# A two-layer encoder trunk on one core: the first layer's attention as one pipeline of paired heads

## The reference

```python
h = x @ w_in
q_lat, ckv, krope, g_mla, dq, dk, dv, g_diff = split(h)       # 256, 128, 32, 512, 512, 512, 512, 512 columns
q = (rmsnorm(q_lat) @ w_uq)                                    # 8 latent heads of 64 + 32 (rope)
ckv = rmsnorm(ckv); krope = rope(krope); dq, dk = rope(dq), rope(dk)
# latent attention, 8 heads: softmax(q_abs . ckv + q_rope . krope) @ ckv, then @ w_uv
# differential attention, 4 heads with two maps each:
a = softmax(q1 . k1) - lam * softmax(q2 . k2);  o_diff = rmsnorm(a @ v) * (1 - lam_init)
o = concat([o_mla * silu(g_mla), o_diff * silu(g_diff)]) @ w_out
y = layernorm(ALPHA * x + o)
```

## Time and profile before

| | |
|---|---|
| time, median of 3 runs (lowest, highest) | 985.28 us (981.5, 987.18) |
| the profiled execution: time, span | 975.73 us, 973.9 us |
| mean granted TensorE clock | 0.957 |
| PE, DVE, ACT, POOL busy (share of the span) | 90%, 58%, 41%, 6% |
| the chain that ended last: PE, issue, DVE, ACT | 64%, 20%, 6%, 4% |
| DMA, mean | 88 GB/s |

### The profile page before, as it was taken

The page is one execution under the profiler, slowest core; times in us unless marked ns, Lnnn a source line. Parts: engine busy times, 40 slices in busy tenths (PEclk is TensorE's granted clock), DMA queues, the critical chain, the costliest instruction groups (busy, mean ns, idle before and its releaser), DMA issues.

```text
span 973.9 us, 17284 instructions
## 1 busy us (share of the span) xinstructions
PE 881.3 (90%) x6744; PEld 745.6 (77%) x6744; DVE 561.7 (58%) x1189; ACT 398.3 (41%) x836; POOL 54.3 (6%) x75
## 2 busy tenths in 40 slices
PE   4897989999998998998989999999999999898975
PEld 3896568788877765786779999888888888766653
DVE  3166533644462676557595246657656666778867
ACT  3232331222232443424113265566557555755520
POOL 0001000000000000000022001000100010000001
PEclk9899979899999998999999999999999999999978
DMA  7232010211224234014203333323332343234301
GB/s 252 67 87 62 1 55 29 67 37 40 71 66 153 71 114 127 24 46 152 83 25 103 107 112 101 121 85 113 116 110 89 110 121 115 63 101 135 97 38 70
DMA packets 70606, 86.14 MB, mean 88 GB/s; under 512 B 8208, under 2 KB 57120, under 8 KB 70528
## 3 DMA queue, kind: packets, MB, share of 16 engines
q1 hardware_dynamic: 67632, 76.76, 25.7%
q0 software_dynamic: 2896, 8.28, 2.4%
HBM read 74.12 MB, written 10.90 MB: 87 GB/s over the span
## 4 chain that ended last, share of the span: by engine, by line
PE 64%; issue 20%; DVE 6%; ACT 4%; SPq 2%; POOL 2%; DMA 2%; DVEq 0%; POOLq 0%; ACTq 0%
PE turn L858 21%; PE pair L858 19%; PE proj L858 9%; PE value L858 9%; PE turn L896 1%; POOL rstd L831 1%; DVE w_lo L1439 1%; PE turn L1064 1%; PE value L896 1%; DMA stage<-in_w_out_even_dram 1%; PE pair L896 1%; SPq L678 1%; ACT w_hi L1247 1%; PE proj L896 1%; DMA stage<-in_w_in_even_dram 1%
## 5 line engine op out<-in xcount | busy, mean ns | idle before, releaser
L1439 DVE TENSOR_TENSOR w_lo<-stage,w_hi 128x512 fp32r<-128x512 f32 (+1 forms) x144 | 96.7, 683 | 149.8 <-ACT w_hi L1247 149.1
L858 PE MATMUL turn<-w_hi,xT_hi 128*128 128x256 f32 (+2 forms) x430 | 137.6, 320 | 4.8 <-DVE xT_lo L1444 1.8
L858 PE MATMUL turn<-w_lo,xT_hi 128*128 128x256 f32 (+2 forms) x430 | 133.1, 309 | 0.0
L858 PE MATMUL turn<-w_hi,xT_lo 128*128 128x256 f32 (+2 forms) x430 | 132.8, 309 | 0.0
L1247 ACT CAST w_hi<-stage 128x512 fp32r<-128x512 f32 (+1 forms) x144 | 86.7, 616 | 47.9 <-DMA stage<-in_w_in_even_dram 14.9
L858 PEld LDWEIGHTS turn<-w_hi,xT_hi 128*128 128x128 f32 x430 | 85.1, 198 | 10.0 <-DVE xT_lo L1444 2.1
L858 PEld LDWEIGHTS turn<-w_hi,xT_lo 128*128 128x128 f32 x430 | 84.8, 197 | 3.6
L858 PEld LDWEIGHTS turn<-w_lo,xT_hi 128*128 128x128 f32 x430 | 85.1, 198 | 2.9
L858 PE MATMUL pair<-w_hi,xT_hi 128*128 128x256 f32 (+2 forms) x196 | 59.8, 305 | 9.9 <-DVE w_lo L1439 9.9
L1317 ACT ACTIVATE probs<-pair,stats 128x272 f32<-128x272 f32 (+4 forms) x64 | 33.1, 518 | 86.9 <-DVE stats L1547 86.6
L1558 DVE TENSOR_TENSOR_SCAN probs<-probs 128x512 f32<-128x512 f32 (+4 forms) x80 | 60.9, 794 | 1.6
(11 more groups left out here) (509 smaller groups left out, 2099.7 us busy)
## 6 DMA issues: line engine op xcount, KB each, us to landing
stage<-in_w_in_odd_dram SPq DMA_DIRECT2D x64, 256.0 KB, 2.7
stage<-in_w_in_even_dram SPq DMA_DIRECT2D x44, 256.0 KB, 2.8
k_c<-in_cache_sb_k_dram SPq DMA_DIRECT2D x32, 256.0 KB, 3.4
v_c<-in_cache_sb_v_dram SPq DMA_DIRECT2D x32, 256.0 KB, 2.9
x_sb<-in_x_prompt_dram SPq DMA_DIRECT2D x8, 512.0 KB, 4.4
mlaK<-in_cache_diff_k_dram SPq DMA_DIRECT2D x8, 512.0 KB, 3.7
mlaK<-in_cache_diff_v_dram SPq DMA_DIRECT2D x8, 512.0 KB, 4.5
stage<-in_w_out_even_dram SPq DMA_DIRECT2D x16, 256.0 KB, 2.9
```

Of the source, the lines that this page charges most:

```text
L858: return nc.tensor.matmul(o, l, r, start=first, stop=last)
L1439: v.tensor_tensor(piece(w_lo[:, sec % 2, words]), piece(stage[:, n % STAGES, :]), piece(w_hi[:, sec % 2, words].bitcast(F32)), ALU.subtrac ...
```

## The change

- The two pipelines become one, `softmax_pipeline`: 16 steps ("M", tile, pair of heads) with 8 MS, then 16 D with 8 DS. In turn i PE does `score` of step i, then `turn` and `value` of step i-1, with a fill of projections between them; `weigh`, which is DVE's part after the exponentials, comes last in the turn. The fills are written out turn by turn.
- A D step scores both maps in one job into the two banks of a pair; one maximum over both; the two maps' weights are mixed in one pass and the scale is applied to the 128 columns of the value.
- An M step does two heads. Their weights are divided by the row sums before the transposes (two passes, which are new); `value` comes out transposed, 64 rows per head side by side, into `o_mT` on ACT. `G` is made transposed too, so the latent half of the output needs no `ogT`; `mcvt` splits `o_mT` to high and low.
- SiLU becomes x times (tanh(x/2) + 1)/2: one Tanh on ACT and one or two DVE instructions.
- The opening: x's transposes, conversions and first `A` products are interleaved; the order of sections is A, dv, dk, dq, G, gd; `kn` and `dv` products lie between `uq` and `qT`; ACT copies the rotary key; the small loads go to POOL's queue, the cached latents behind `rms`.
- Layer 0 uses layer 1's division of the banks from its first score on, and eight banks in rotation before it.

```diff
-    for i in range(turns):
-        if i < len(steps):
-            jobs.append(("score", steps[i]))
-            if steps[i][0] == "D":
-                jobs.append(("score2", steps[i]))
...
-        if 2 <= i < len(steps) + 2:
-            jobs.append(("turn", steps[i - 2]))
...
-            jobs.append(("value", steps[i - 3]))
+    for i, now in enumerate(steps):
+        fill = fills.get(i, [])
+        jobs.append(("score", now))
+        for bundle in fill[:-1]:
+            jobs += bundle
+        if i:
+            jobs += weighted(steps[i - 1])
+        for bundle in fill[-1:]:
+            jobs += bundle
+        for j in samples:
+            if i == max([j - 2, 0] + [k for k in samples if k < j]):
+                jobs += [("cacheT",) + steps[j] + (k,) for k in range(2)] if steps[j][0] == "DS" else [("cacheT",) + steps[j]]
+        jobs += later.pop(i, [])
+        if i:
+            s = steps[i - 1]
+            jobs.append(("value", s))
...
+        jobs.append(("weigh", now))
...
+    jobs = layer0(0) + first[0:2] + layer0(1) + first[2:4] + [("A", 0, 0)]
+    jobs += layer0(2) + second[0:1] + [("A", 1, 0)] + layer0(3) + second[1:2] + [("A", 2, 0)]
+    jobs += layer0(S_TILE) + second[2:3] + [("A", 3, 0)] + second[3:4] + [("A", S_TILE, 0)]
+    jobs += flat_jobs(beside([[("A", t, 1)] for t in tiles], convert("dv0"))) + [("rms",)]
+    jobs += flat_jobs(beside([[("dv", t, 0)] for t in tiles], convert("dv1")))
+    jobs += [("lam",)] + [("latT", t) for t in tiles]
+    values = beside([[("dv", t, 1)] for t in tiles], convert("dk0"))
...
+    steps = mingle([("M", t, pair) for pair in range(MH // 2) for t in (3, 0, 2, 1)], [("MS", b) for b in range(STREAMS)])
+    fills = {i: [[("dk", i // 2, i % 2)] + ([("dkT", i // 2 - 1)] if i % 2 and i > 1 else [])] for i in range(2 * TILES)}
...
+    for i in range(8):
+        fills[24 + i] = [[("G", i // 2, i % 2)]]
...
+                        for i in range(2):
+                            r = slice(HD * i, HD * i + HD)
+                            mm(o[:, i, 0:n], dqT[r, h, tok(t)], dkT[r, h, 0:n], True, False)
+                        for i in range(2):
+                            m = mm(o[:, i, n - P:n], identb[:, :], mask_chunk[:, :], False, True)
...
-                            m = mm(o[:, 0:MV], w[:, tok(j)], vm[:, j, h * MV:(h + 1) * MV], j == 0, j == last)
+                                m = mm(o[MV * i:MV * i + MV, 0:P], vm[:, j, h * MV:(h + 1) * MV], wT[:, i, tok(j)], j == 0, j == last)
...
-                    nc.scalar.activation(rot[:, job[1] % 2, :], ps(job)[:, :], ACT.Silu).then_inc(done, 1)
+                    nc.scalar.activation(gtmp0[n % 2][:, 0:m], ps(job)[:, 0:m], ACT.Tanh, scale=0.5).then_inc(tanh_done, 1)
...
+                    if s[0] in ("M", "MS"):
+                        for i in range(m):
+                            e = v.tensor_scalar(prob(s, i), prob(s, i), coef[:, r, i:i + 1], None, ALU.mult)
...
+                        v.scalar_tensor_tensor(out=prob(s, 0), in0=prob(s, 1), scalar=coef[:, r, 2:3], in1=prob(s, 0),
                                                op0=ALU.mult, op1=ALU.add).then_inc(weigh_done, 1)
```

More of the change, by code:

```diff
@@ L59, with softmax_pipeline, weighted @@
 QUAD = 2 * NEW
[L64 to L82, removed]
[L83 to L98 removed]
+def softmax_pipeline(steps, fills, after):
+    jobs, later = [], {}
+    samples = [j for j, s in enumerate(steps) if s[0] in ("MS", "DS")]
+    def weighted(s):
+        return [("turn", s)] + ([("turn2", s)] if s[0] == "M" else [])
+    for i, now in enumerate(steps):
[14 more added lines that the diff above has]
+            jobs.append(("value", s))
+            for turns_on, job in after(s):
                 later.setdefault(i + turns_on, []).append(job)
[L100 to L102 removed]
+        jobs.append(("weigh", now))
     return jobs
@@ L212, in make_schedule, with layer0 @@
     tiles = range(TILES)
-    jobs = [("xT", 0, t, h) for t in tiles for h in range(2)] + convert("A0", "A1")
-    jobs += [("A", t, 0) for t in tiles]
-    jobs += flat_jobs(beside([[("A", t, 1)] for t in tiles], convert("G0"))) + convert("G1") + [("rms",)]
-    jobs += [("G", t, 0) for t in tiles]
-    jobs += flat_jobs(beside([[("G", t, 1)] for t in tiles], convert("dk0")))
-    jobs += [("latT", t) for t in tiles] + [("lam",)]
+    first, second = convert("A0"), convert("A1")
+    def layer0(t):
+        return [("xT", 0, t, 0), ("xT", 0, t, 1)]
@@ L247, in make_schedule @@
-    jobs += pipeline(
-        steps, fill, "end",
-        ahead=lambda s: [("cacheT",) + s + (k,) for k in range(2)] if s[0] == "DS" else [],
-        after=lambda s: [(1, ("dsT", s[1]))] if s[0] == "DS" else [(1, ("post", s[1]))] if s[2] == DH - 1 else [])
-    jobs += [("gd", S_TILE), ("gate", 3), ("od",)]
-    jobs += flat_jobs(beside([[("ogT", t, 0)] for t in tiles], convert("out000")))
-    jobs += [("out", 0, 0, 0, 0)]
-    jobs += flat_jobs(beside([[("ogT", 0, 1)], [("ogT", 1, 1), ("out", 0, 0, 1, 0)], [("ogT", 2, 1)]], convert("out001")))
@@ new lines, in after @@
+    def after(s):
+        if s[0] == "DS":
+            return [(1, ("dsT", s[1]))]
+        if s == ("MS", STREAMS - 1):
+            return [(1, ("om",))]
+        return [(1, ("post", s[1])), (2, ("norm", s[1]))] if s[0] == "D" and s[2] == DH - 1 else []
+    jobs += softmax_pipeline(steps, fills, after)
+    last = steps[-1]
+    jobs += [("turn", last), ("ogT", 1, 1), ("value", last), ("dsT", STREAMS - 1), ("od",), ("post", 0), ("norm", 0), ("gate", 0)]
+    jobs += [("out", 0, 0, 0, 0), ("post", S_TILE), ("out", 0, 0, 0, 1), ("ogT", 0, 1), ("norm", S_TILE), ("gate", S_TILE)]
@@ L350, in assign_banks @@
 def assign_banks(schedule):
-    pairs = [i for i, j in enumerate(schedule) if j[0] == "score" and j[1][0] in ("B", "BS")]
+    first = next(i for i, j in enumerate(schedule) if j[0] == "score")
     uses, turns, holder, where = {s: 0 for s in SLOTS}, {}, {}, {}
@@ L716, in _ @@
                     load_quarter(job[1] + STAGES)
+                if job == ("rms",):
+                    for b in range(CKV_SLOTS):
+                        sp.dma_start(ckv_c[:, b, :, :], ckv_cache[:, b, :, :]).then_inc(ckv_in[b], 16)
                 if kind == "latT" and job[1] == S_TILE:
```

388 lines of the change are left out of this document (224 added, 164 removed).

## The result

| | time, median (lowest to highest) | ratio to the kernel before, 95% interval |
|---|---|---|
| before | 985.12 us (978.73 to 987.18) | |
| after | 990.93 us (989.62 to 996.99) | 1.0084 (1.0044 to 1.0124) |

The change makes the kernel slower by 0.8% (6 us between the medians); the forecast was 944 us, 4% faster. The profiled execution of after took 990.11 us, its span is 988.3 us (973.9 before) and its mean clock 0.938 (0.957).

A forecast was written before the change was run, and what follows sets the result against it. PE, with holes, was taken to bound layer 0. Gains of 10 (opening), 7.5 (`latT` to `qa`), 18 (pipelines) and 6 (output) sum to 41.5, from 985.3 to 944 us; the 8-in-10 range is 912 to 976.

The forecast's parts named there:

- Stalls in the pipelines: Layer 0's two pipelines: 30 us of stalls over 48 turns plus 12 of clock, 42 against 39.3 before.
- one-turn distance: Rival, merged pipeline: `turn` waits for `weigh` of its step; slower than before, 999 us at 1.8 us a turn; chance 0.13.
- 72 less 48 s: Whole kernel: gain of 72 us without merged-pipeline stalls, less 48 turns times mean stall s; forecast s 0.63.
- The opening: Start to the end of `A`: loads off SP's queue let the fourth weight quarter come earlier; 10 us gain, ends 1 and 13.
- `latT` to `qa`: Stage from 83 to 129 us: ACT copies the rotary key and `dv` products give cover; 7.5 us gain, ends 3 and 11.
- PE work: Two pipelines of layer 0: same projections, shorter D scores and M values; together 21 us less.
- The scores: D steps: two maps' scores overlap, 1.91 to 0.94 us at 384 columns; 14.5 us saved, ends 8 and 16.
- The values: M steps: 40 blocks of two heads at 0.255 us instead of 0.41; 6.3 us saved.
- Tanh: Gates among the exponentials: assumed to load no table; the rival that it does gave 988 us, chance 0.05.
- Holes: Layer 0, first 525 us: PE idle time and clock loss, put at some 60 to 70 us before the change.
- Output stage: End of layer 0: 20 transposes go (2 us) and 4 us of idle; 6 us gain, ends 2 and 10.
- Layer 1: From about 525 us: same code, time taken as unchanged; a move over 3 us would make the forecast wrong.

The follow-up runs named there:

- experiments 1 and 2: experiment 1, and, against the changed kernel, transposes and values two turns behind their score with a third exponentials buffer, division still last: 942.21 us, ratio 0.9609.
- experiment 1: Changed kernel with each layer 0 division ahead of the fill, later jobs and value copy in VectorE's order, instead of last: 943.92 us, ratio 0.9615.
- experiment 9: Changed kernel with eight unread products before each differential-stage wait of the transposes for the division: 985.76 us; the changed kernel rerun unedited: 991.03 us.
- experiment 6: Changed kernel with the small inputs' and cached latents' loads back on SP's queue, ahead of the fourth weight quarter: 1009.21 us, ratio 1.0283.
- Experiment 7: Changed kernel with latent transposes ahead of two `dv1` conversions, `lam` behind them, and sample query transposes ahead of value products: 978.89 us, ratio 0.9994.
- experiment 5: Two maps of each differential score apart again: in the changed kernel 998.42 us; in the kernel with the division ahead of the fill 956.13 us.
- experiment 3, conversions: Changed kernel with each turn's weight conversions moved behind the division in ScalarE's and VectorE's orders: 979.2 us, ratio 0.9982.

## Why the prediction was wrong

**The step that failed** is the one named as the least sure, "Stalls in the pipelines": 30 us of idle and 12 of clock over 48 turns came out as 48.9 and 36.8. The mechanism of the stalls was named there, `weigh` behind the fill's own VectorE work at a distance of one turn, and experiments 1 and 2 show it. The waits for it, 41.6 us, lie even within the 15 to 60 that the forecast allowed them. What failed is the size, and more than half of that in the clock:
- The clock was taken "at 12 us of loss for 17.7 now", from no row, while idle time was forecast to rise. It cost 36.8, 24.8 more. When experiment 1 takes 31 us of idle away, 18 of clock go with them; experiment 9 raises the clock by filling the waits alone. In the earlier trace rows, behind the first stage, the clock is 1.00 only where TensorE never idles.
- The sum over a turn left things out. The latent turns came out near it (13.4 us of waits for the 12 of the rotations), the differential ones not (28.2 for the 18 of the gates). The turn shown has gate and output product (1.0 us), two conversions (1.2), the value copy (0.3) and `weigh` (1.1) behind a wait of 0.7 for the Tanh, together 4.3 us after the fill's end, against 1.8 of cover, the work that TensorE has left in that time. The forecast had 2.4 to 2.8 against 1.2 to 2.0, a stall of 1.0; the conversions it priced only in the rival.
- The remaining 7 us of idle are waits for other work than `weigh`, for which there was no term.

One remedy stood in the text unused: "DVE's order is fixed, `weigh` is always last" is given as a fact, though the order is what experiment 1 changes at no cost.

The rival "one-turn distance" has the outcome right, slower than before, with a chance of 0.13 given to it, but its own measure was not reached. It decides from a mean stall of 1.5 us a turn; measured are 48.9/48 = 1.02 of idle. Only with the clock's 24.8 us on top does its formula, 72 less 48 s, get s = (85.7 - 12)/48 = 1.54. Its reason against itself, "PE's cover is longest where the steps are widest", holds but does not help: the widest steps, of 512 columns, are 8 of 48.

**The opening**: right in size, 10.2 us for 10. That the queue holds the fourth quarter back is shown (experiment 6), but the division of the gain is another than forecast: with the new order in place the queue is worth 18 us of the opening, and the order without it costs 7.8. The small loads on POOL's queue left 0.93 us of wait for the fourth quarter; the first `A` product, with this wait in it, ends near 16.6 us, for 17 forecast. (The loads taken off SP's queue are 16, not 15.) The Trainium skill, "DMA: Bandwidth & Descriptors", section "SWDGE vs HWDGE vs iDMA", has the two queues take turns; by that the term was 8 instead of 10, and no run here shows these 2 us.

**`latT` to `qa`**: wrong in sign, +3.4 for -7.5. A part of it is a misread row: 83 to 129 us was taken as the stage, but its last 3.8 us belonged to the pipeline, which starts at 125.2. The rest is 5.87 us ahead of `uq` and 3.0 ahead of `qa`. Ahead of `uq` VectorE converts a quarter that landed late until 63.2 us, makes the constants of `lam` until 65.6, and only then copies what TensorE waits for; ahead of `qa` ScalarE's copies stand behind a conversion that waits 1.0 us for its quarter. Experiment 7 takes both away and is worth 9 us; its stage takes 50.0 us, 6.5 less than before by the same sum, near the 7.5 forecast. The forecast's check, `uq` within 5 us of the last `latT`, fails with 6.9.

**PE work**: without its holes the two stages took 306.3 - 41.3 = 265.0 us before and 332.4 - 85.7 = 246.7 after, 18 less for 21 forecast. The scores gave 12.6 of their 14.5 (experiment 5): the step of 384 columns is as the earlier trace rows said, but the mean over the four widths is 0.83 us for the 0.9 taken. That the mask product "stands once for both" is a misreading: it is made once for each map, after as before (x2 in the line of experiment 5), and both rows that were compared hold both of them, so the sum does not suffer. The values' 6.3 us were not measured by themselves. **Tanh**: no table is loaded for it, as taken; the Trainium skill, "ScalarE: Activation LUTs", section "Table sets: the hidden batching unit", agrees. **Holes**: those listed from 17.3 us on add up to 71 us, not to "60 to 70". **Output stage**: 8.2 for 6. **Layer 1**: 3.3 us longer with the same code, just over the 3 us that the forecast allowed itself; the same code took 456 to 460 us in the profiles of the other kernels here, so before's 454.8 is the shortest of all. Why is open.

So the kernel slower than before was one order of jobs away from the forecast: with the division ahead of the fill it takes 943.9 us, for 944 forecast. That is partly luck: the holes of the pipelines are 36.6 us there for the 42 forecast, while the stage from `latT` on still gives nothing of its 7.5 us.

## What to carry to other kernels

When a pipeline's distance is shortened, write down for each turn what stands ahead of the critical operation in its engine's order, what each of these waits for itself, and compare the sum with the cover turn by turn. An operation on which TensorE waits belongs ahead of work that nobody waits for, even where its engine is busy half of the time only. Charge idle TensorE twice: for its length, and for the clock that falls with it. In the two pipeline stages here 49 us idle came with 37 us of clock (changed kernel), 18 with 19 (experiment 1) and 42 with 22 (experiment 3, conversions): idle time and clock fell together, but not in a fixed proportion.

## What was not expected of the hardware

- Work without use raised the clock enough to pay for itself: 192 products in the waits of a stage, clock 0.87 to 0.95, stage 170.6 to 168.0 us, one execution each (experiment 9).
- The clock fell to 0.87 over a stage whose longest single wait is 3.1 us. After the 14.75 us stop of experiment 6 the next 6.4 us had a clock of 0.64, the products starting 0.21 us apart at first (0.37 for the first one) where they start 0.12 apart at 2.4 GHz.
- Issuing is not free on SP's queue: two loads of cached latents occupy it for 6.65 us (8.24 in before), and a weight quarter behind them that every further product waits for is issued that much later.
